# Pair-adding the squares of six norms on GpSimd in a two-block transformer trunk

## The reference, cut to what matters

```python
for l in range(2):
    h = rms_norm(x, mix_pre_g[l])
    ...                                  # h @ w_in, attention groups, gated unit
    mix = concat([out_a, out_b, out_c]) @ w_mix_out[l]
    x = x + rms_norm(mix, mix_post_g[l])
    h = rms_norm(x, mem_pre_g[l])
    x = x + rms_norm(memory_cross_attention(h, mem_n, ...), mem_post_g[l])
    h = rms_norm(x, ffn_pre_g[l])
    x = x + rms_norm(conv_ffn(h, ...), ffn_post_g[l])
# rms_norm(v, g) = v * rsqrt(mean(v * v, over the 1024 channels) + eps) * g
```

## Time and profile before

| | us |
|---|---|
| median of 3 runs | 1927.75 |
| lowest and highest | 1924.67, 1928.99 |
| the profiled execution | 1928.05 |
| its span, first to last instruction | 1926.2 |
| TensorE busy | 1820.8 (95%), 10394 matmul records |
| VectorE busy | 522.7 (27%) |
| ScalarE busy | 429.1 (22%) |
| GpSimd busy | 74.6 (4%), 72 instructions |
| mean granted TensorE clock | 0.971 |

### The profile page before, as it was taken

The page is one execution under the profiler, slowest core; times in us unless marked ns, Lnnn a source line. Parts: engine busy times, 40 slices in busy tenths (PEclk is TensorE's granted clock), DMA queues, the critical chain, the costliest instruction groups (busy, mean ns, idle before and its releaser), DMA issues.

```text
span 1926.2 us, 25090 instructions
## 1 busy us (share of the span) xinstructions
PE 1820.8 (95%) x10394; PEld 1413.9 (73%) x10394; DVE 522.7 (27%) x1141; ACT 429.1 (22%) x925; POOL 74.6 (4%) x72
## 2 busy tenths in 40 slices
PE   6969898799999999999899999999999999899997
PEld 3665676566566666678678888888886688788886
DVE  3779441410000000022421212221234312212113
ACT  2542221111011110121542221111224522211112
POOL 0251000100000000010000100000000000000000
PEclk9889798899999999999999999999999999899999
DMA  9101178199999999973313324444443132234420
GB/s 394 42 22 66 54 276 333 77 398 422 422 422 422 422 422 422 422 305 138 130 66 132 109 110 150 152 151 152 140 137 131 47 128 110 88 134 152 155 84 22
DMA packets 53645, 383.32 MB, mean 199 GB/s; under 512 B 6208, under 2 KB 6336, under 8 KB 7360
## 3 DMA queue, kind: packets, MB, share of 16 engines
q1 hardware_dynamic: 52272, 376.97, 50.1%
q10 hardware_dynamic: 1296, 5.24, 0.7%
HBM read 381.14 MB, written 1.05 MB: 198 GB/s over the span
## 4 chain that ended last, share of the span: by engine, by line
PE 88%; DVE 8%; ACT 3%; issue 1%; DMA 1%; ACTq 0%; DVEq 0%
PE ps L575 84%; DVE arena L1962 3%; PE ps L573 2%; DVE ring L1956 1%; PE ps L632 1%; DVE arena L1956 1%; DVE arena L1959 1%; DMA ipos<-in_pos 1%; ACT arena L1720 1%; DVE small L2429 0%; DVE ring L2095 0%; DVE arena L2327 0%; ACT L1455 0%; DVE arena L1970 0%; ACT arena L1828 0%
## 5 line engine op out<-in xcount | busy, mean ns | idle before, releaser
L575 PE MATMUL ps<-arena,ring 128*128 128x256 f32 (+2 forms) x3680 | 832.5, 387 | 9.1 <-DVE arena L1962 3.9
L575 PEld LDWEIGHTS ps<-arena,ring 128*128 128x128 f32 x3680 | 694.8, 192 | 135.7 <-issue 42.4
L575 PE MATMUL ps<-ring,arena 128*64 128x256 f32 (+4 forms) x3168 | 484.2, 418 | 0.0
L575 PEld LDWEIGHTS ps<-ring,arena 128*64 128x64 f32 (+1 forms) x3168 | 292.9, 148 | 175.2 <-issue 87.2
L575 PE MATMUL ps<-arena 128*128 128x128 f32 (+5 forms) x1256 | 202.2, 322 | 6.6 <-DVE rounds_i L2283 1.8
L575 PEld LDWEIGHTS ps<-arena 128*128 128x128 f32 (+3 forms) x1256 | 166.8, 189 | 37.5 <-issue 22.8
L1962 DVE SCALAR_TENSOR_TENSOR arena<-ps,par,arena 128x255 f32<-128x255 f32 (+1 forms) x178 | 74.3, 480 | 336.5 <-ACT arena L1932 335.6
L575 PE MATMUL ps<-ring 128*128 128x256 f32 (+2 forms) x896 | 116.1, 301 | 8.9 <-DVE ring L2113 7.8
L575 PEld LDWEIGHTS ps<-ring 128*128 128x128 f32 (+2 forms) x896 | 98.5, 163 | 22.8 <-issue 10.1
L1932 ACT ACTIVATE arena<-ps,par 128x256 f32<-128x256 f32 x88 | 42.4, 562 | 313.6 <-PE ps L575 313.6
L575 PE MATMUL ps<-arena,cst 128*128 128x256 f32 (+1 forms) x308 | 91.2, 442 | 11.7 <-ACT arena L1748 5.4
(11 more groups left out here) (176 smaller groups left out, 852.0 us busy)
## 6 DMA issues: line engine op xcount, KB each, us to landing
ring<-in_stream SPq DMA_DIRECT2D x358, 1024.0 KB, 10.4
arena<-in_xc ACTq DMA_DIRECT2D x1, 1024.0 KB, 5.3
xT<-in_xc ACTq DMA_DIRECT2D x1, 1024.0 KB, 8.8
arena<-in_mem ACTq DMA_DIRECT2D x1, 1024.0 KB, 4.9
out_y<-xT ACTq DMA_DIRECT2D x2, 512.0 KB, 2.7
ring<-in_dft ACTq DMA_DIRECT2D x1, 512.0 KB, 8.0
arena<-in_sguw ACTq DMA_DIRECT2D x2, 256.0 KB, 2.9
par<-in_par SPq DMA_DIRECT2D x1, 511.5 KB, 24.6
```

The lines of the kernel that those rows point to most:

```text
L575: i = nc.tensor.matmul(out, lhsT, rhs, start=start, stop=stop, skip_group_check=skip)
```

## The change

The norms 2, 4, 6, 8, 10 and 12 sum four tiles on TensorE in place of eight. GpSimd adds tiles 2 and 3 of the squares to tiles 0 and 1 (one 128x512 addition, once the squares of step 1 are there), then tiles 4 and 5 to the same (once those of step 2 are there, and the first addition is through), and signals `norm_pairs`. TensorE sums tiles 0, 1, 6, 7. It no longer does so between the steps of the projection but all at once in the gap, behind the first filling job where there is one. The norm 0 and the odd ones stay as they are.

```diff
+        xp_ok = sem("norm_pairs")
...
             mem_gain(memn, 0)
-            pool.wait_ge(late_ps, LATE_JOBS["kv_end0"])
-            mem_gain(memn, 1)
+
+            def pair_sums(k):
+
+                for c in (2, 4):
+                    pool.wait_ge(xq_ok, 8 * k + c + 2)
+                    i = tt(sq[:, 0:2, :], sq[:, 0:2, :], sq[:, c:c + 2, :], ALU.add)
+                    if c == 2:
+                        link(i)
+                i.then_inc(xp_ok, 1)
+
+            for k in range(2, 1 + 6 * LAYERS, 2):
+                pair_sums(k)
+                if k == 2:
+                    pool.wait_ge(late_ps, LATE_JOBS["kv_end0"])
+                    mem_gain(memn, 1)
...
-            def sums(k, chunks):
+            def sums(k):
 
-                for c in chunks:
-                    pe.wait_ge(xq_ok, 8 * k + c + 1)
+                for c in range(KC) if k % 2 or k == 0 else (0, 1, 6, 7):
+                    if k % 2 or k == 0 or c > 1:
+                        pe.wait_ge(xq_ok, 8 * k + c + 1)
+                    else:
+                        pe.wait_ge(xp_ok, k // 2)
                     mm(bank(3, T), ones, sq[:, c, :], c == 0, c == KC - 1, xs_ps if c == KC - 1 else None)
...
                     release()
-                    if n:
-                        sums(k, (2 * n - 2, 2 * n - 1))
...
-                sums(k, (6, 7))
+                sums(k)
...
-                        if i == FFN_PAIRS - 1 and o % 2 and o > 1:
-                            sums(n0 + 5, (o - 3, o - 2))
...
-                    sums(n0 + 5, (6, 7))
+                    sums(n0 + 5)
```

More of the change, by code:

```diff
@@ L1150, in gap @@
                     mem_kv(l, fill[0])
-                sums(k, (6, 7))
+                sums(k)
                 if l < LAYERS:
                     mem_kv(l, fill[1])
-                sums(k + 1, range(KC))
+                sums(k + 1)
                 if l < LAYERS:
@@ L1158, in _ @@
             mem_kv(0, 1, memn0, 1)
-            sums(0, range(KC))
+            sums(0)
             mem_kv(0, 1, memn0, 1)
-            sums(1, range(KC))
+            sums(1)
             mem_kv(0, KV_START - 2, memn0, 1)
```

## The result

The changed kernel took 1910.43 us (median of 4 runs, 1909.03 to 1911.13) against 1926.21 us (median of 4, 1922.06 to 1928.99). The ratio is 0.992, interval 0.9906 to 0.9934, so it is faster, by 0.8%.

What follows compares the result with a forecast made beforehand. The prediction took TensorE alone, busy 95% of the span, as the bound. 12 pairs x 0.86 = 10.3 us off the profiled 1928.05 us, all else 0, gave 1917.7, stated as 1917.5 us; range 1914 to 1921.3.

Steps and rivals of the forecast that it cites:

- Part 1: TensorE at six norms: two pairs of summing matmuls fewer each, 1.72 us, 10.3 us in all; moving the rest costs nothing.
- Part 2: Behind the projection: in norms 2, 4, 6, 8 job and root come 0.86 us earlier, costed at nothing.
- Part 3: Twelve GpSimd additions, 1.2 us each, hidden at no cost; slack 8.0 us in norms 2, 4, 8; norm 12 narrowest.
- Part 4: GpSimd's queue and VectorE: additions ahead of the second layer's gains move nothing, and the engines do not meet in memory.
- The Sum: Whole kernel: 10.3 us off for removed matmuls, 0 for additions, waits and moved pairs, giving 1917.5 us.
- Rival (a): TensorE's clock gives some back or adds some: 3.5 us either way, 1914 or 1921 us; chance 0.17.
- (b): Slow additions make TensorE wait: 1932.5 us at 6 us each, slower by over 0.2% from 5.9; chance 0.03.
- (c): Gain mostly lost, through additions of 4.1 to 5.9 us or matmuls already covered by weight waits: 1925 us; chance 0.05.
- (d): The edit does not do what it says, for instance sums still take eight tiles; chance 0.

Runs made afterwards that it cites:

- r3: Kernel before plus the twelve GpSimd additions into a place nobody reads, TensorE waiting for them, all eight matmuls kept: 1925.61 us, ratio 1.0005.
- r2: Kernel before with all eight summing matmuls moved into the gap behind the projection, no additions: 1922.15 us, ratio 0.9995.
- r4: Changed kernel without the additions, TensorE summing only tiles 0, 1, 6 and 7: 1910.02 us, ratio 0.9932 to the kernel before.
- r6: Changed kernel with each of the twelve additions followed by four idle copies of itself: 1934.86 us, ratio 1.0053 to the kernel before.
- r9: The changed kernel a third time, nothing further edited: 1909.13 us, ratio 0.9927 to the kernel before.
- r1: The changed kernel again, with more runs of the kernel before beside it: 1911.88 us, ratio 0.9942.
- r8: Changed kernel with further GpSimd additions in norms 2, 4, 6 and 8, so TensorE sums one tile there: 1905.21 us, ratio 0.9896 to before.
- r12: The r8 kernel again (one tile for TensorE in norms 2, 4, 6 and 8): 1910.53 us, ratio 0.9941 to the kernel before.

## Why the prediction was wrong

**Part 1** was right in its sum: 1.72 us for each of the six norms in every trace of the changed kernel, 10.3 in all, and r3 shows that the additions alone do nothing. That the change of place costs TensorE nothing is right too. It isn't worth nothing everywhere, though: in norms 10 and 12, where no job stands behind the projection, the root waits for the squares and the table load, and there r2's move alone gives 0.6 and 1.0 of the 1.72 us.

**Part 2** was right: the root of the filled norms comes 0.8 us earlier, and nothing follows from it (71.06 us from norm 2 to 4, as before).

**Part 3** was right. An addition takes 1.27 us (1.2 taken). Slack 7.9 us in norm 2 (8.0 forecast); a wait in norm 12 of 0.83 us on the loads (0.65 forecast), hidden behind the table load; r4 without additions runs in the same time. The rule of the Trainium skill, "GPSIMD Engine Reference", section Engine selection, that such an addition belongs on VectorE, has its ratio right (1.27 against 0.69 us), and it did not matter, as the text had it.

**Part 4** was right: the gains of the second layer start at 1057.60, still released by TensorE.

**The Sum** is the step that failed, in two ways. *Its starting point*: it took 1928.05 us, one execution, and three runs around it. Over 91 runs the kernel before has a mean of 1924.6 us, with single runs from 1914.8 to 1929.7; the profile lay in the upper part. From the mean the same sum gives 1914.3 us, just inside the range. *Its last term*: waits and moved work at 0 was true of instructions and not of the clock, whose effect on the time it left at 0. The changed kernel's mean over 16 runs is 1910.7 us, 13.9 below (about 1.2 either way, if the runs are independent). So of the 7.1 us between the forecast and the measured 1910.43 us, 3.2 are the starting point and 3.6 the gain beyond the matmuls (the rest is the scatter of four runs). Of the 13.9 us, 10.3 are the matmuls and about 1.7 the way from norm 6 to norm 8, with 3.4 us less at the lower clock. From norm 10 to norm 12 the time is either 241 or 237.8 us, in both kernels: 241 in 5 of the 6 traces with nothing or 3.45 us removed in the first layer, in 2 of the 7 with 1.72 or 5.17. If these shares were exact, that would be another 1.8 us and the sum complete (13.8); with so few traces the shares are only argued.

**Rival (a)** named the cause, with a chance of 0.17, and got its reach about right (3.5 us either way; the means differ by 3.6 more than the matmuls), but not its places. It looked at norm 10 alone. There its 10.4 us at the lower level are right (10.2 in the clock's record), and the most they moved the time is 3.3 us. Two traces of the same kernel differ by 9.7 us, 6.3 of them ahead of norm 2, and a part that comes with the edit every time, 1.7 us, sits in the attention of the second layer, a stretch that the earlier trace rows don't hold. The Trainium skill, "TensorE: Matmul & The Clock Gate", section What's actually happening, says that the gate's watch runs freely and that its phase when a kernel starts makes the kernel's beginning vary from run to run; the traces agree (first square of norm 2 anywhere from 1012.8 to 1024.2 us). The prediction drew from it that this part would vary anyway. That was half of it: with the program shortened by 1.7 us at norm 2, the low stretch behind it changed every time in the same way.

**Rivals (b), (c), (d)**: none happened. r6 shows the places of (b) and its waits nearly as worked out, and the slow clock after a wait in addition: at 6.7 us an addition costs 24 us and not 18. So (b)'s price is too low for such waits, and its threshold of 5.9 us is likely too high.

Why does the time from norm 6 to norm 8 depend on the shift and not on where the trace began? The program has fallen into step with the clock's changes by the end of the first block. The stretch at full clock (1.00) ahead of norm 2 shows it, from the end of the last low one to the first square, in before and r9 and then in after:

```profile
970.99:1022.54 51.55, 50.48 (x242) 39.54 (x241) 10.26 (x32) 17.00 (x49) 0.00 (x0) 1.00 0.23 82
969.50:1021.08 51.58, 50.51 (x242) 39.56 (x241) 10.26 (x32) 17.04 (x50) 0.00 (x0) 1.00 0.24 82
...
938.65:1017.88 79.23, 74.23 (x372) 56.90 (x371) 22.68 (x66) 34.26 (x94) 0.00 (x0) 1.00 0.22 80
```

It is 51.5 to 51.6 us long in 14 of the 18 traces and 79.2 in the other four (after, r1, r8, r12), though the square itself stands anywhere within 11.4 us. The three traces of the kernel before all have 51.6 us; the changed kernel, the same up to here, has 51.6 twice and 79.2 twice. So the edit moves a program that comes to norm 2 in one of two positions against the clock's changes, and that tells the last pieces apart too. Of the six traces with 5.17 us removed the two with 79.2 us have 240.8 us from norm 10 to norm 12, the four with 51.6 us 237.8. What stays open is how the program falls into step, why it does so in two positions, and how often in each. No run here changes the clock by itself.

## What to carry to other kernels

Where TensorE's stream has no gap, count removed matmuls by the spacing of the weight loads; it was exact to a hundredth here. A GpSimd addition cost nothing where TensorE asked for it later than it ended. It cost nothing in norm 12 either, where TensorE waited and the root waited longer for its table load. When a run tests a move, measure from ahead of the first moved instruction: from the last square on r2 seemed to lose 0.8 us in norm 12, and it gained 1.0. Start the sum from a median over many runs, and before giving a range compare two profiles of the unedited kernel piece by piece: two traces of one and the same program differed here by 9.7 us, nearly what the edit gives. Test an edit in parts of different size: a gain that doesn't grow with the part removed is not all the removed work's.

## What the runs showed of the hardware that was not expected

The clock turned a smooth gain into a stepped one: 1.72, 3.45 and 5.17 us of removed matmuls gave 3.5, 3.5 and 6.9 us by norm 8, and the kernel with norm 2 alone edited is as fast as the one with two norms edited (1919.7 and 1921.1 us). The traces tie this to the clock: 6.8 us at the lower level between norm 6 and norm 8, or 3.4. And in all 18 traces the program came to norm 2 in one of two positions against the clock's changes, wherever it had begun. A TensorE that waited 7.3 us ran its next four matmuls in 3.8 us where 1.99 is usual, at a granted clock of 0.50, and lost another 5.5 us beyond its wait before norm 8.
